# Earlier short-convolution taps, earlier bonus sums and earlier first statistics in a hybrid RWKV-7 / attention / PEER step

## The chip, the cores and the metric

The kernel runs on one core of one Trainium2 chip. The metric is the device time of one execution in microseconds (us). The kernel before was timed three times: 3184.2, 3185.47 and 3186.89 us, a median of 3185.47 us. One more execution was recorded by the hardware profiler, and all rows below come from it.

The engines are TensorE (PE, matmuls, with its weight loads shown as PEld), VectorE (DVE), ScalarE (ACT), GpSimd (POOL) and SyncE (SP). Each executes its own instructions in program order. They wait for each other through semaphores: `then_inc(name, 1)` counts up when an instruction is done, and `wait_ge(name, n)` holds an engine until the count is reached.

## The reference

One step of a two-layer model for 128 context tokens and 256 latent tokens of width 1024. Layer 0 mixes tokens with a bidirectional RWKV-7 scan beside a short gated convolution, layer 1 with differential attention. Each mixer is followed by a PEER expert retrieval. The parts that the change touches are these:

```python
def short_conv(bg, cg, hc, conv_w):
    z = cg * hc
    zp = jnp.pad(z, ((0, 0), (1, 1), (0, 0)))
    y = zp[:, 0:T] * conv_w[0] + zp[:, 1:T + 1] * conv_w[1] + zp[:, 2:T + 2] * conv_w[2]
    return bg * y

# in rwkv7_bidir, for each of the two directions d
kd = heads(k * (1 + (a - 1) * k_a))
s_fin, o = wkv_scan(s0[:, d], rh, decay, kd, vh, kk, heads(a), d == 1)
bons.append(jnp.sum(rh * kd * r_k.astype(f32), axis=-1, keepdims=True) * vh)
# after both: group norm of the outputs, plus bons[0] + bons[1], times the gate

# around the mixer
hp = rmsnorm(xp, norm_mix[l]) * (1 + sc1p) + sh1p      # the same for xs
xp = xp + g1p * yp
hp = rmsnorm(xp, norm_ffn[l]) * (1 + sc2p) + sh2p      # statistics of the updated x
xp = xp + g2p * peer(hp, peer_w_q[l], ...)
```

## The kernel before, in words

The 384 tokens are three tiles of 128 (t = 0 context, t = 1 and 2 latent). All weights pass through one SBUF ring of four slots, 512 KB a tile, in a fixed order that SP follows. SP reloads a slot when its tile is used: for tiles that are split in a high and a low part (input projection, query, experts) when DVE has made the low part (`low`), for the others when PE has multiplied them. `high(g)` on ACT waits for the landing of tile g and copies it to `w_hi`, and `low(g)` on DVE makes the rest `w_lo`.

Layer 0 goes through these stages:

- The input projection of 26 column bands (`project`, `take_projection`). For each band PE does 24 matmuls, and ACT copies the result to `proj`. Between bands, ACT, DVE and PE run the pieces of `rwkv_prep(n)`, which makes decays, normalised keys and the vectors KAP, BET, GAM, RHO of both directions. ACT calls its piece n after taking band n, DVE calls its piece n after `low` of band n. The bands come in the order `MIX0`, which ends with `CG`, `HC` (the convolution's inputs), `BG` and the gate's lora band.
- The scan (`rwkv_units`). There are six units q (a direction and a token tile each). In each, `levels(q)` inverts a triangular system in six levels lv. At each level PE makes a product, DVE masks it (`PM`), PE multiplies again, DVE subtracts from `XM` and transposes it, and the next level can start. The function `between(q, lv, s)` on every engine hangs other work into this chain at step (lv, s): the matrices of the next unit, pairs of adaLN weight tiles on PE (`ada_pair`), and in unit 0 the short convolution and the bonus.
- The output rows (`even_rows`) on PE, the residual updates (`after_mix`) on DVE, and on ACT the sums of squares for the next norm (`norm_stats_by_half`), which visits six half tiles in the order `ROWS_MIX[0]`: (0,0), (1,0), (0,1), (0,2), (1,1), (1,2) as (half nb, tile t). DVE needs the root of tile 0 for `normalise(1, 0)`, which it calls ahead of the third residual.
- The second norm: PE transposes `xn` (`norm_T`), ACT and DVE scale and split it (`norm_evac`), the query projection follows, then the experts.

The convolution before is made in unit 0: DVE's product z = CG * HC at step (1,0), ACT's centre tap at (1,1), DVE's first outer taps at (2,0), its second outer taps at (4,2), and the product with BG at (5,2). The bonus sum kd[0] + kd[1], times r, is made by DVE at (1,2) and scaled by r_k on ACT at (2,0); PE needs it at (4,0).

Of the kernel before, what the change touches and what calls it, by code (L numbers as in the profile page):

```python
# [21 lines left out]
ALU = mybir.AluOpType  # L22
ACT = mybir.ActivationFunctionType
AX_X = mybir.AxisListType.X

P = 128
# [7 lines left out]
NF = 4  # L34
# [94 lines left out]
def build(nc, A):  # L129
    with ExitStack() as ctx:  # L130
# [1106 lines left out]
        def _(act):  # L1237
# [30 lines left out]
            def norm_stats_by_half(n, rows):  # L1268

                seen = set()  # L1270
                for k, (nb, t) in enumerate(rows):
                    cols = slice(512 * nb, 512 * nb + 512)
# [48 lines left out]
            def rwkv_prep(n):  # L1321
# [31 lines left out]
                if 12 <= n < 18:  # L1353
# [7 lines left out]
                    if k == 2:  # L1361
                        act.activation(dec[d], half[d], ACT.Exp, scale=-c).then_inc(exp_ready, 1)

            def rwkv_units():
# [12 lines left out]
                def between(q, lv, s):  # L1377

                    at = (lv, s)
                    if q == 0 and at == (1, 1):  # L1380
                        act.wait_ge(conv_z, 1)
                        for f in range(NF):
                            act.activation(proj[:, HC + f, :], proj[:, CG + f, :], ACT.Copy, scale=ft("conv", 4 + f)).then_inc(conv_y, 1)
                    if q == 0 and at == (2, 0):
                        act.wait_ge(rkd_sum, 1)
                        for f in range(NF):
                            ins = act.activation(kd[0][:, f, :], kd[0][:, f, :], ACT.Copy, scale=ft("r_k", f))
                        ins.then_inc(rkd_ready, 1)
# [171 lines left out]
            for layer in range(2):  # L1560
# [12 lines left out]
                for n in range(2):  # L1573
                    high(at["query"] + n)
                norm_stats_by_half(2 * layer + 1, ROWS_MIX[layer])
# [10 lines left out]
        def _(dve):  # L1586
# [143 lines left out]

            def rwkv_prep(n):
# [61 lines left out]
                if n in (21, 24):  # L1793
                    rho_kappa((n - 21) // 3)

            def rwkv_units():
# [146 lines left out]
                def taps(w, lo):  # L1943

                    z, y = proj[:, CG:CG + NF, :], proj[:, HC:HC + NF, :]
                    for f in range(NF):
                        for a, b in ((0, P), (P, T)):
                            out = y[:, f, a + 1:b] if lo else y[:, f, a:b - 1]
                            src = z[:, f, a:b - 1] if lo else z[:, f, a + 1:b]
                            ins = dve.scalar_tensor_tensor(out, src, ft("conv", w + f), out, ALU.mult, ALU.add)  # L1950
                    chained(ins)

                def short_conv(at):

                    z, y = proj[:, CG:CG + NF, :], proj[:, HC:HC + NF, :]
                    if at == (1, 0):
                        tt(z, z, y, ALU.mult).then_inc(conv_z, 1)
# [527 lines left out]
```

## Time and profile before

| quantity | value |
|---|---|
| median of three runs | 3185.47 us |
| profiled execution, whole time | 3189.87 us |
| its span (first to last instruction) | 3188.0 us |
| PE busy | 3065.4 us, 96% |
| DVE busy | 2029.4 us, 64% |
| ACT busy | 1147.5 us, 36% |
| mean granted TensorE clock | 0.988 of full |

The profiled execution took 4.40 us longer than the median of the runs, and its span leaves out 1.87 us of it. Times of rows are us from the start of the span. In the rows of instructions in order of time, a bracket is the idle time of the engine ahead of the group and what ended it. The input projection ends at about 167 us, unit 0 of the scan reaches to about 214 us, the scan to about 435 us, and the query projection of layer 0 starts at about 480 us.

### The profile page before, as it was taken

What the parts mean: (1) busy time and instruction counts of PE and PEld (TensorE: products, weight loads), DVE (VectorE), ACT (ScalarE), POOL (GpSimd) and SP (SyncE); (2) the same over time, 40 slices, a digit from 0 to 9 for tenths busy, and PEclk for the clock granted to TensorE, in tenths of its full rate; (3) what the DMA queues carried; (4) which work ended last, traced back from release to release, by engine and by line L of the source; (5) the groups of instructions that cost most, each with busy time, mean ns of one, the idle gap of its engine ahead of it and who ended that gap; (6) DMA issues with size and microseconds to landing.
All of it is one profiled execution on the core that took longest, in us unless ns stands there. A gap on an engine that the chain in (4) does not pass through costs nothing.

```text
span 3188.0 us, 51951 instructions
## 1 busy us (share of the span) xinstructions
PE 3065.4 (96%) x20266; PEld 2689.6 (84%) x20266; DVE 2029.4 (64%) x4372; ACT 1147.5 (36%) x1552; POOL 11.2 (0%) x23
## 2 busy tenths in 40 slices
PE   7989889999999999999999979999999999999998
PEld 4956649999999998888888868999999998888887
DVE  3875554687878436666666474587878625666666
ACT  4611113454545432222223264345454532222222
POOL 0000000000000000000000000000000000000000
PEclk9999999999999999999999989999999999999999
DMA  6345533566665856766763313456565765766763
GB/s 229 112 160 205 184 119 124 155 207 192 201 196 189 285 159 204 235 214 211 237 206 122 111 46 120 127 180 214 178 218 181 232 226 179 237 213 211 238 204 132
DMA packets 281942, 589.16 MB, mean 185 GB/s; under 512 B 17744, under 2 KB 181712, under 8 KB 275360
## 3 DMA queue, kind: packets, MB, share of 16 engines
q1 hardware_dynamic: 140960, 428.57, 40.8%
q10 hardware_dynamic: 139008, 151.00, 14.3%
q0 software_dynamic: 1792, 7.01, 0.6%
q8 instruction: 132, 2.16, 0.3%
q14 instruction: 50, 0.41, 0.0%
HBM read 482.97 MB, written 103.55 MB: 184 GB/s over the span
## 4 chain that ended last, share of the span: by engine, by line
PE 88%; DVE 7%; DMA 2%; issue 1%; ACT 1%; SPq 0%; ACTq 0%; DVEq 0%
PE ps L1182 33%; PE ps L580 13%; PE ps L582 13%; PE ps L581 13%; PE ps L1158 4%; DVE arena L1596 3%; DMA ring<-in_ada 2%; PE ps L553 1%; PE ps L690 1%; PE ps L641 1%; DVE w_lo L1596 1%; PE ps L1131 1%; PE ps L672 1%; PE ps L757 1%; PE ps L607 0%
## 5 line engine op out<-in xcount | busy, mean ns | idle before, releaser
L1596 DVE TENSOR_TENSOR w_lo<-ring,w_hi 128x1024 fp32r<-128x1024 f32 x576 | 702.2, 1221 | 344.9 <-ACT w_hi L1251 344.0
L580 PE MATMUL ps<-hT_hi,w_hi 128*128 128x384 f32 x2576 | 873.5, 339 | 3.0 <-ACT arena L1524 3.0
L581 PE MATMUL ps<-hT_lo,w_hi 128*128 128x384 f32 x2576 | 861.4, 334 | 0.0
L582 PE MATMUL ps<-hT_hi,w_lo 128*128 128x384 f32 x2384 | 797.8, 335 | 0.0
L1251 ACT ACTIVATE w_hi<-ring 128x1024 fp32r<-128x1024 f32 x378 | 400.0, 1060 | 964.6 <-PE ps L582 791.9
L1182 PE MATMUL ps<-w_lo,ga_hi 128*128 128x512 f32 x1512 | 596.6, 395 | 0.0
L1182 PE MATMUL ps<-w_hi,ga_lo 128*128 128x512 f32 x1512 | 596.6, 395 | 0.0
L1182 PE MATMUL ps<-w_hi,ga_hi 128*128 128x512 f32 x1512 | 596.6, 395 | 0.0
L580 PEld LDWEIGHTS ps<-hT_hi,w_hi 128*128 128x128 f32 x2576 | 484.1, 188 | 6.4 <-issue 5.9
L1544 ACT ACTIVATE w_hi<-ring 128x1024 fp32r<-128x1024 f32 x224 | 238.2, 1063 | 697.9 <-PE ps L1182 634.5
L1596 DVE TENSOR_TENSOR arena<-arena 128x768 bf16<-128x768 bf16 (+10 forms) x937 | 422.6, 511 | 99.5 <-PE ps L1158 94.3
L581 PEld LDWEIGHTS ps<-hT_lo,w_hi 128*128 128x128 f32 x2576 | 484.5, 188 | 0.5
L582 PEld LDWEIGHTS ps<-hT_hi,w_lo 128*128 128x128 f32 x2384 | 448.0, 188 | 0.0
L2306 DVE CAST ga_hi<-xn 128x384 fp32r<-128x384 f32 x256 | 92.5, 361 | 423.4 <-PE ps L1182 408.1
L1182 PEld LDWEIGHTS ps<-w_hi,ga_lo 128*128 128x128 f32 x1512 | 284.9, 188 | 66.5
L1182 PEld LDWEIGHTS ps<-w_lo,ga_hi 128*128 128x128 f32 x1512 | 284.9, 188 | 66.4
L1182 PEld LDWEIGHTS ps<-w_hi,ga_hi 128*128 128x128 f32 x1512 | 284.9, 188 | 66.3
L1508 ACT ACTIVATE arena<-ps 128x512 f32<-128x512 f32 x192 | 192.5, 1105 | 1.4 <-PE ps L1158 1.0
L1158 PE MATMUL ps<-arena 128*128 128x128 bf16 x2304 | 150.8, 219 | 6.1 <-DVE arena L1596 5.6
L1158 PEld LDWEIGHTS ps<-arena 128*128 128x128 bf16 x2304 | 133.1, 97 | 23.1 <-issue 14.2
L1596 DVE TENSOR_TENSOR ga_lo<-xn,ga_hi 128x384 fp32r<-128x384 f32 x256 | 143.0, 559 | 8.9
L1596 DVE TENSOR_TENSOR xn<-arena 128x384 f32<-128x384 f32 (+2 forms) x274 | 147.4, 541 | 0.3
(313 smaller groups left out, 2147.9 us busy)
## 6 DMA issues: line engine op xcount, KB each, us to landing
ring<-in_u SPq DMA_DIRECT2D x256, 512.0 KB, 3.8
ring<-in_v SPq DMA_DIRECT2D x256, 512.0 KB, 3.4
ring<-in_ada SPq DMA_DIRECT2D x96, 512.0 KB, 4.8
act_dram<-arena SPq DMA_DIRECT2D x256, 192.0 KB, 3.9
g_dram<-arena ACTq DMA_DIRECT2D x48, 1024.0 KB, 4.1
arena<-g_dram ACTq DMA_DIRECT2D x32, 1536.0 KB, 9.6
arena<-act_dram ACTq DMA_DIRECT2D x32, 1536.0 KB, 15.6
ring<-in_mix_in SPq DMA_DIRECT2D x42, 512.0 KB, 3.3
```

Of the source, the lines that this page charges most:

```text
L553: mm = pe.matmul(ps[g:g + 8, 6, :], silu8[:, c, b, :], w[:, 512 * cc:512 * cc + 512], start=(b == 0 and c < 4), stop=(b == 3 and c >= 4))
L580: pe.matmul(out, hi[:, c, :], hT_hi[:, c, :], start=(c == 0), stop=False)
L581: pe.matmul(out, hi[:, c, :], hT_lo[:, c, :], start=False, stop=False)
L582: mm = pe.matmul(out, lo[:, c, :], hT_hi[:, c, :], start=False, stop=(c == DC - 1))
L641: mm = pe.matmul(ps[:, 3 * nb + t, :], l_[:, c, ts], r_[:, cc, :], start=(c == 0 and m == 0), stop=(c == DC - 1 and m == 2))
L1158: mm = pe.matmul(ps[:, k, q * P:(q + 1) * P], hot_u[n % 3][:, q // 2, :, q % 2], gated_hot[n % 3][:, q // 2, w, :, q % 2], start=(w == 0), ...
L1182: mm = pe.matmul(ps[:, 2 * t + nb, :], l_[:, n % 2, ts], r_[:, cs], start=(first and q == 0), stop=False, skip_group_check=True)
L1251: act.activation(w_hi[:, g % WB, :], ring[:, g % RING, :], ACT.Copy).then_inc(hi_ready, 1)
L1508: act.activation(gstage[:, b, :, 4 * q:4 * q + 4].rearrange("p j t -> p t j"), ps[:, k, :].rearrange("p (t j) -> p t j", t=4), ACT.Copy).t ...
L1544: act.activation(w_hi[:, g % WB, :], ring[:, g % RING, :], ACT.Copy).then_inc(hi_ready, 1)
L1596: return dve.tensor_tensor(out, a, b, op)
L2306: dve.tensor_copy(ga_hi[:, k % 2, :], ga[:, k % 2, :]).then_inc(ga_high, 1)
```

## The change

Three things move. No operation is added or removed.

1. The convolution's product z, its centre tap and its first outer taps leave unit 0 and become pieces of `rwkv_prep`: DVE makes z in piece 24 and the taps in piece 25, ACT makes the centre tap in piece 23.
2. The bonus sums leave unit 0 as well: DVE makes them in piece 25, and ACT scales them in piece 24.
3. In layer 0, ACT takes the statistics of tile 0 first, and copies the first two query tiles (`high`) behind them. In layer 1 the order stays.

```diff
-            def norm_stats_by_half(n, rows):
+            def norm_stats_by_half(n, rows, highs_at=None, highs=()):
                 seen = set()
                 for k, (nb, t) in enumerate(rows):
+                    if k == highs_at:
+                        for g in highs:
+                            high(g)
...
+                if n == 23:
+                    act.wait_ge(conv_z, 1)
+                    for f in range(NF):
+                        act.activation(proj[:, HC + f, :], proj[:, CG + f, :], ACT.Copy, scale=ft("conv", 4 + f)).then_inc(conv_y, 1)
+                if n == 24:
+                    act.wait_ge(rkd_sum, 1)
+                    for f in range(NF):
+                        ins = act.activation(kd[0][:, f, :], kd[0][:, f, :], ACT.Copy, scale=ft("r_k", f))
+                    ins.then_inc(rkd_ready, 1)
...
-                    if q == 0 and at == (1, 1):
-                        act.wait_ge(conv_z, 1)
...
-                    if q == 0 and at == (2, 0):
-                        act.wait_ge(rkd_sum, 1)
...
-                for n in range(2):
-                    high(at["query"] + n)
-                norm_stats_by_half(2 * layer + 1, ROWS_MIX[layer])
+                norm_stats_by_half(2 * layer + 1, ROWS_MIX[layer], 0 if layer else 2, [at["query"], at["query"] + 1])
...
+                if n == 24:
+                    dve.wait_ge(proj_taken, 21)
+                    tt(proj[:, CG:CG + NF, :], proj[:, CG:CG + NF, :], proj[:, HC:HC + NF, :], ALU.mult).then_inc(conv_z, 1)
+                if n == 25:
+                    chained(tt(kd[0], kd[0], kd[1], ALU.add))
+                    tt(kd[0], kd[0], proj[:, R_:R_ + NF, :], ALU.mult).then_inc(rkd_sum, 1)
+                    dve.wait_ge(conv_y, NF)
+                    taps(0, 1)
...
-                    if at == (1, 0):
-                        tt(z, z, y, ALU.mult).then_inc(conv_z, 1)
-                    if at == (2, 0):
-                        dve.wait_ge(conv_y, NF)
-                        taps(0, 1)
...
-                        if at == (1, 2):
-                            chained(tt(kd[0], kd[0], kd[1], ALU.add))
-                            tt(kd[0], kd[0], proj[:, R_:R_ + NF, :], ALU.mult).then_inc(rkd_sum, 1)
```

The first place is the end of the projection. On DVE, before, the last low part (`w_lo_m`) is the last work ahead of the scan, whose first instruction writes `gate_bc`:

```order
L1596 TENSOR_TENSOR w_lo_m<-ring,w_hi 128x1024 [waits hi_ready]
L1596 TENSOR_TENSOR arena<-arena 128x1536 [waits proj_taken]
L1596 TENSOR_TENSOR arena<-arena,xn 128x1536
L1596 TENSOR_TENSOR w_lo_m<-ring,w_hi 128x1024 [waits hi_ready]
L1596 TENSOR_TENSOR gate_bc<-const 128x64 [waits prep_done,levels_in,proj_taken]
```

Now z stands ahead of that low part, and the bonus sums (written to `xn`) and eight tap instructions, of which the first two are shown, stand behind it:

```order
L1597 TENSOR_TENSOR w_lo_m<-ring,w_hi 128x1024 [waits hi_ready]
L1597 TENSOR_TENSOR arena<-arena 128x1536 [waits proj_taken]
L1597 TENSOR_TENSOR arena<-arena,xn 128x1536
L1597 TENSOR_TENSOR arena<-arena 128x1536 [waits proj_taken]
L1597 TENSOR_TENSOR w_lo_m<-ring,w_hi 128x1024 [waits hi_ready]
L1597 TENSOR_TENSOR xn<-xn,arena 128x1536
L1597 TENSOR_TENSOR xn<-xn,arena 128x1536 [waits dve_order]
L1739 SCALAR_TENSOR_TENSOR arena<-arena,feats 128x127 [waits conv_y]
L1739 SCALAR_TENSOR_TENSOR arena<-arena,feats 128x255
```

On ACT at the same place, now, the two groups of four scalings stand between the copies of the last bands (L1320 takes a band, L1387 is the scan's first work):

```order
L1320 ACTIVATE arena<-ps 128x384 [waits multiplied] x2
L1369 ACTIVATE arena<-arena,feats 128x384 [waits conv_z]
L1369 ACTIVATE arena<-arena,feats 128x384 x3
L1320 ACTIVATE arena<-ps 128x384 [waits multiplied]
L1373 ACTIVATE xn<-xn,feats 128x384 [waits rkd_sum]
L1373 ACTIVATE xn<-xn,feats 128x384 x3
L1320 ACTIVATE arena<-ps 128x384 [waits multiplied]
L1387 ACTIVATE arena<-ps 128x512 [waits turn_ready,proj_taken]
```

Before, the same stretch of ACT had only the copies of the bands, and the scalings came in the scan (`ACT L1383`, `L1387`).

The second place is unit 0 of the scan on DVE, from the masked product of level 1 to the subtraction of level 2 (`hslab` holds the unit's matrices). Before:

```order
L1596 TENSOR_TENSOR arena<-ps,gate_bc 128x128 [waits fill_ready] x2
L1596 TENSOR_TENSOR arena<-arena 128x1536
L1596 TENSOR_TENSOR hslab<-hslab,ps 128x64x2 [waits fill_ready] x2
L2055 STREAM_TRANSPOSE hslab<-hslab 128x256 [waits fill_taken]
L2058 STREAM_TRANSPOSE hslab<-hslab 64x256 [waits fill_taken]
L2058 STREAM_TRANSPOSE hslab<-hslab 64x256
L1596 TENSOR_TENSOR xn<-xn,arena 128x1536
L1596 TENSOR_TENSOR xn<-xn,arena 128x1536 [waits dve_order]
L1596 TENSOR_TENSOR arena<-ps,gate_bc 128x128 [waits fill_ready] x2
L1950 SCALAR_TENSOR_TENSOR arena<-arena,feats 128x127 [waits conv_y]
```

Now:

```order
L1597 TENSOR_TENSOR arena<-ps,gate_bc 128x128 [waits fill_ready] x2
L1597 TENSOR_TENSOR hslab<-hslab,ps 128x64x2 [waits fill_ready] x2
L2055 STREAM_TRANSPOSE hslab<-hslab 128x256 [waits fill_taken]
L2058 STREAM_TRANSPOSE hslab<-hslab 64x256 [waits fill_taken]
L2058 STREAM_TRANSPOSE hslab<-hslab 64x256
L1597 TENSOR_TENSOR arena<-ps,gate_bc 128x128 [waits fill_ready] x2
L1597 TENSOR_TENSOR hslab<-hslab,ps 128x32x4 [waits fill_ready] x2
```

Nothing but the chain of the levels is left between the two subtractions.

The third place is ACT between the end of the scan (the root of the last group norm) and the third half tile's statistics. Before, the two copies of query tiles (`w_hi<-ring`) come first:

```order
L1427 ACTIVATE xn<-ps,feats 128x512 [waits gn_ready]
L1251 ACTIVATE w_hi<-ring 128x1024 [waits multiplied,weight_landed2]
L1251 ACTIVATE w_hi<-ring 128x1024 [waits multiplied,weight_landed3]
L1275 ACTIVATE xn,stat<-x 128x512 [waits x_updated]
L1278 ACTIVATE stat<-stat,feats 128x1 [waits act_order]
L1275 ACTIVATE xn,stat<-x 128x512 [waits x_updated,act_order]
L1280 ACTIVATE stat<-stat 128x1 [waits act_order]
```

Now the four instructions on tile 0 come first:

```order
L1430 ACTIVATE xn<-ps,feats 128x512 [waits gn_ready]
L1278 ACTIVATE xn,stat<-x 128x512 [waits x_updated]
L1281 ACTIVATE stat<-stat,feats 128x1 [waits act_order]
L1278 ACTIVATE xn,stat<-x 128x512 [waits x_updated,act_order]
L1283 ACTIVATE stat<-stat 128x1 [waits act_order]
L1251 ACTIVATE w_hi<-ring 128x1024 [waits multiplied,weight_landed2]
L1251 ACTIVATE w_hi<-ring 128x1024 [waits multiplied,weight_landed3]
```

The landings of two query tiles are no longer waited for ahead of tile 0's root, but still ahead of the statistics of tiles 1 and 2.

## Rows read from the trace of the kernel before

**Rows 1.** The page's chain that ended last, by engine, shares of the span.

```profile
PE 88%; DVE 7%; DMA 2%; issue 1%; ACT 1%; SPq 0%; ACTq 0%; DVEq 0%
```

**Rows 2.** DVE in order of time, projection's end: start, us, instructions, idle before.

```profile
155.13 1.75 DVE L1596 TENSOR_TENSOR arena<-arena,xn 128x1536 f32<-128x1536 f32 x1
156.80 1.22 DVE L1596 TENSOR_TENSOR w_lo_m<-ring,w_hi 128x1024 fp32r<-128x1024 f32 x1
167.41 0.22 DVE L1596 TENSOR_TENSOR gate_bc<-const 128x64 f32<-128x64 f32 x1 [9.39 <-ACT arena L1317]
```

**Rows 3.** ACT in order of time, last band and the scalings.

```profile
166.89 0.49 ACT L1317 ACTIVATE arena<-ps 128x384 f32<-128x384 f32 x1 [3.67 <-PE ps L582]
...
179.68 2.13 ACT L1383 ACTIVATE arena<-arena,feats 128x384 f32<-128x384 f32 x4 [6.19 <-DVE arena L1596]
184.95 2.13 ACT L1387 ACTIVATE xn<-xn,feats 128x384 f32<-128x384 f32 x4 [3.14 <-DVE xn L1596]
```

**Rows 4.** DVE in order of time, unit 0, levels 1 and 2.

```profile
177.89 1.75 DVE L1596 TENSOR_TENSOR arena<-arena 128x1536 f32<-128x1536 f32 x1
179.56 0.48 DVE L1596 TENSOR_TENSOR hslab<-hslab,ps 128x128 f32<-128x128 f32 x2
...
181.37 3.55 DVE L1596 TENSOR_TENSOR xn<-xn,arena 128x1536 f32<-128x1536 f32 x2
184.84 0.48 DVE L1596 TENSOR_TENSOR arena<-ps,gate_bc 128x128 f32<-128x128 f32 x2
185.24 2.70 DVE L1950 SCALAR_TENSOR_TENSOR arena<-arena,feats 128x127 f32<-128x127 f32 x8
187.97 0.48 DVE L1596 TENSOR_TENSOR hslab<-hslab,ps 128x128 f32<-128x128 f32 x2
```

**Rows 5.** PE in order of time, unit 0, levels 1 to 3.

```profile
178.12 0.67 PE L817 MATMUL ps<-arena,hslab 64*64 64x32 f32 x32 [1.13 <-DVE arena L1596]
180.18 0.67 PE L804 MATMUL ps<-hslab 64*64 64x32 f32 x32 [1.39 <-DVE hslab L1596]
180.78 1.86 PE L553 MATMUL ps<-ring,gate_bc 128*8 128x512 f32 x8
185.42 1.08 PE L817 MATMUL ps<-arena,hslab 64*64 64x32 f32 x32 [2.78 <-DVE arena L1596]
...
193.52 0.67 PE L817 MATMUL ps<-arena,hslab 64*64 64x32 f32 x32 [0.64 <-DVE arena L1596]
```

**Rows 6.** The chain that ended last, in order of time: start, us, what.

```profile
191.72 4.76 DMA ring<-in_ada
```

**Rows 7.** Stretches: length, PE, PEld, DVE, ACT, POOL busy (instructions), PEclk, DMA share, GB/s.

```profile
181.00:191.00 10.00, 7.22 (x68) 3.60 (x60) 9.81 (x20) 3.54 (x7) 0.00 (x0) 0.50 0.30 107
468.00:477.00 9.00, 3.28 (x16) 3.28 (x16) 7.57 (x16) 5.33 (x15) 0.00 (x0) 0.50 0.35 117
```

**Rows 8.** ACT in order of time, after the scan of layer 0.

```profile
461.14 1.06 ACT L1251 ACTIVATE w_hi<-ring 128x1024 fp32r<-128x1024 f32 x1 [2.43 <-DMA ring<-in_query]
...
463.92 0.29 ACT L1280 ACTIVATE stat<-stat 128x1 f32<-128x1 f32 x1
```

**Rows 9.** DVE in order of time, residuals and norm.

```profile
464.32 0.16 DVE L1620 RECIPROCAL stat<-stat 128x1 f32<-128x1 f32 x1 [10.11 <-ACT stat L1280]
...
465.31 0.68 DVE L1596 TENSOR_TENSOR arena<-ps,gate_bc 128x512 f32<-128x512 f32 x1
...
474.29 0.88 DVE L1624 TENSOR_SCALAR xn<-x,stat 128x512 f32<-128x512 f32 x2
```

**Rows 10.** PE in order of time, output rows, transposes, first query matmul.

```profile
443.95 20.77 PE L672 MATMUL ps<-ring,arena 128*128 128x512 f32 x48
465.06 1.09 PE L595 MATMUL ps<-const,xn 128*128 128x128 f32 x8 [0.34 <-DVE xn L1624]
473.72 3.65 PE L595 MATMUL ps<-const,xn 128*128 128x128 f32 x16 [7.57 <-DVE xn L1624]
479.62 0.44 PE L607 MATMUL ps<-hT_hi,w_hi 128*128 128x384 f32 x1 [2.25 <-DVE hT_lo L1596]
```

More of the change, by code:

```diff
@@ L1379, in between @@
                     at = (lv, s)
-                    if q == 0 and at == (1, 1):
-                        act.wait_ge(conv_z, 1)
-                        for f in range(NF):
-                            act.activation(proj[:, HC + f, :], proj[:, CG + f, :], ACT.Copy, scale=ft("conv", 4 + f)).then_inc(conv_y, 1)
-                    if q == 0 and at == (2, 0):
-                        act.wait_ge(rkd_sum, 1)
-                        for f in range(NF):
-                            ins = act.activation(kd[0][:, f, :], kd[0][:, f, :], ACT.Copy, scale=ft("r_k", f))
-                        ins.then_inc(rkd_ready, 1)
                     if q == 3 and at == (4, 0) or q == 5 and at == (3, 0):
@@ L1729, in low, with taps @@
                 tt(lo, ring[:, g % RING, :], hi.bitcast(F32), ALU.subtract).then_inc(lo_ready[TILES[g][0]], 1)
+            def taps(w, lo):
+                z, y = proj[:, CG:CG + NF, :], proj[:, HC:HC + NF, :]
+                for f in range(NF):
+                    for a, b in ((0, P), (P, T)):
+                        out = y[:, f, a + 1:b] if lo else y[:, f, a:b - 1]
+                        src = z[:, f, a:b - 1] if lo else z[:, f, a + 1:b]
+                        ins = dve.scalar_tensor_tensor(out, src, ft("conv", w + f), out, ALU.mult, ALU.add)
+                chained(ins)
             def rwkv_prep(n):
@@ L1941, in bonus @@
                     tt(proj[:, R_ + f, :], filled()[:, 0:T], proj[:, V_ + f, :], ALU.mult).then_inc(fill_taken, 1)
[L1943 to L1951, printed above, removed]
-                def short_conv(at):
-                    z, y = proj[:, CG:CG + NF, :], proj[:, HC:HC + NF, :]
-                    if at == (1, 0):
-                        tt(z, z, y, ALU.mult).then_inc(conv_z, 1)
-                    if at == (2, 0):
-                        dve.wait_ge(conv_y, NF)
-                        taps(0, 1)
+                def short_conv(at):
                     if at == (4, 2):
@@ L1963, in short_conv @@
                     if at == (5, 2):
-                        tt(proj[:, BG:BG + NF, :], proj[:, BG:BG + NF, :], y, ALU.mult).then_inc(conv_done, 1)
+                        tt(proj[:, BG:BG + NF, :], proj[:, BG:BG + NF, :], proj[:, HC:HC + NF, :], ALU.mult).then_inc(conv_done, 1)
                 def between(q, lv, s):
```

## The prediction

> **What bounds the kernel now.** I read the page's chain of waits first: PE carries 88% of it, DVE 7% and DMA 2% [rows 1]. So a DVE or ACT instruction only counts where PE stands idle for it. The changed code runs in two such places, and I read each in order of time on PE, DVE and ACT.
>
> In unit 0 of the scan DVE is never idle between 177.9 and 188 us, while PE has gaps of 1.39 and 2.78 us that DVE ends [rows 4, 5]. In the 10 us from 181 to 191, DVE is busy 9.81 us and PE 7.22, at a granted clock of 0.50, the lower level of 1.2 GHz [rows 7]. DVE bounds this stretch, and the work to be moved stands in it. Ahead of it, at the end of the projection, DVE is idle for 9.39 us until ACT has taken the last band [rows 2].
>
> After the scan DVE is idle for 10.11 us until ACT has made tile 0's root, and ACT got to it late because its copy of the second query tile waited for the landing until 461.14 [rows 8, 9]. PE finishes the output rows at 464.72 and then has a gap of 7.57 us between the transposes of tile 0 and those of tile 1 [rows 10].
>
> **Part 1, where the work goes to.** DVE's z takes 1.67 us of its time (177.89 to 179.56), the bonus sums 3.47 (181.37 to 184.84), the taps 2.73 (185.24 to 187.97), in all 7.87 us [rows 4]. At the projection's end, z now starts at 156.80 and ends at 158.5, and the last low part follows at 158.5 to 159.6. PE needs that one at 162.7 (one band's 4.16 us ahead of the last band's end, 3.67 + 0.49 in [rows 3]), so 3 us are left. The bonus sums run to about 163.1 (+3.5) and the taps to 165.8 (+2.7), where DVE's first scan instruction could not start before 167.41 anyway [rows 2]. The 9.39 us of idle time hide the 7.87, with 1.6 us to spare.
>
> ACT has two groups of four scalings of 2.13 us each [rows 3]. Bands are taken at 158.57, 162.73 and 166.89 (4.16 apart). The first group follows band 23's copy at 159.05, when z is ready since 158.5, and ends at 161.2, ahead of band 24. The second waits for the bonus sums at 163.1, just when band 24's copy is done (163.2), and ends at 165.4, 1.5 us ahead of the last band. Behind that wait stands the copy of the last band, and PE, DVE and ACT all start the scan on it. Beyond 1.5 us, each us of delay would cost one. I cost this at nothing.
>
> **Part 1, what it removes.** All else up to PE's product at 178.12 stays. It ends at 178.79, and DVE can subtract at 178.83 instead of 179.56 [rows 4, 5]. From there to the next DVE step behind the transposes it is 1.81 us (179.56 to 181.37), so the transposes end at 180.6. PE's next product starts at 179.45 (0.14 behind the subtraction's end, as 180.18 stands behind 180.04) and its pair of adaLN tiles at 180.05. DVE's masked product of level 2 starts at 180.6 instead of 184.84 and ends at 181.1. PE's second product then starts at 181.2 to 181.4 instead of 185.42, which the idle 2.78 us and the DVE work before it had held.
>
> From here the price depends on PE's clock. The product took 1.08 us at the lower level, and 0.67 at the full one [rows 5]. DVE's subtraction of level 2 starts at 181.9 (full) or 182.4 (half) instead of 187.97, 6.0 or 5.5 us earlier. To PE's product of level 3 at 193.52 it is 5.55 us of DVE work in both. The second brake is the ring: the transfer in the chain takes 4.76 us from 191.72, behind the second pair of tiles, and ends in a PE start at about 196.5 [rows 6]. That pair would be done at 184.6 instead of 191.3 with the full clock (6.7 earlier), at about 186 with half the clock for a few us (5.3), and at about 187 if the level stayed low as long after PE has become dense as before (from 185.42 to 191, [rows 5, 7]), which gives 4.2. Upper end 6.0, lower end 4.2. Before the drop PE now has the adaLN pair and two products close together, so I expect a shorter stretch at half clock, but not none: I take 5.2 us. Behind level 3 the order is as before, so the scan shifts by this as a whole, its own transfers with it.
>
> **Part 2.** The first two residuals are done at 454.21 (464.32 less 10.11 idle, [rows 9]). ACT's statistics of one half tile take 1.05 us (463.92 + 0.29 less the second copy's end at 462.1, halved, [rows 8]), so tile 0's root is ready at 455.4. PE does six output tiles in 20.77 us, 3.46 each [rows 10]: the fourth is half done at 456.0 and done at 457.8, the sixth done at 464.72. DVE therefore normalises tile 0 at 456.0 (1.0 us), and the residuals three and four (1.35 us each, 465.31 less 464.32 being the norm's 0.99) end at 459.8.
>
> The query copies on ACT wait for the same landings as before: at 457.65 (the copy that ended at 458.71 took 1.06) and 461.14 [rows 8]. DVE's low parts follow at 459.8 and 462.2, the second ending at 463.4. Residual five (PE's part is there at 463.0) ends at 464.8, residual six waits for PE's 464.72 and ends at 466.2. ACT has done the statistics three and four at 464.2, takes five at 464.8 and six at 466.2, ready at 467.3. DVE's last normalisation then starts at 467.5 instead of 474.29 and ends at 468.4: 6.8 us earlier. What is late next is no longer a landing but PE's own last output tile, with a tail of residual, square, root and scaling.
>
> PE gains a little more. Its 16 transposes took 3.65 us at a clock of 0.50, 0.228 each, against 1.09 us for 8 before it, 0.136 each [rows 7, 10], and DVE waited for them. With PE's idle stretches now about 1 us between tile 0's and tile 1's transposes, they should run at the full clock, and DVE can scale at once behind its own normalisation: 469.15, split 1.6 us later, low part 0.9, first query matmul at 471.8 instead of 479.62, that is 7.8 us. Lower end: the clock still falls, and besides the first query matmuls run at half clock for about the 3.7 us of dense work that it took to rise (473.72 to some 477.4, [rows 7, 10]), losing 1.85, and the transposes 0.2: 5.8. I take 7.8.
>
> A rule speaks against this. In [rows 7, 10] PE did nothing but transposes from 473.72 on, and by 478 the clock was full when the first query matmul came at its usual pace. The Trainium skill, "TensorE: Matmul & The Clock Gate", section "Part 4: PE-mode transpose", says that transposes don't count as busy time for the clock in the same way as matmuls; by it, PE would look idle from 464.72 to 471.8 and the gain would be the 5.8 us. The rows side with the transposes counting.
>
> **The sum.** 5.2 + 7.8 = 13.0 us. The profiled execution's 3189.87 us becomes 3176.9; against the median, which is 4.40 us lower, 3185.47 becomes 3172.5 us. All that follows (experts, layer 1) is the same order of work, started earlier. Three runs lay within 2.7 us, so 0.2% (6.4 us) is about what can be told from no change.
>
> **The rivals.**
> - *The ring takes the scan's gain back.* For: a transfer of 4.76 us is in the chain of unit 0 [rows 6], and with less DVE work the same tiles are wanted faster. Against: the next pairs keep their distance, since the order behind level 3 is unchanged. If the tiles pace unit 0, part 1 is worth 1 us: 3185.47 - 8.8 = 3176.7. Chance 0.13.
> - *The clock falls at the query projection after all.* Part 2 is worth 5.8: 3174.5. Chance 0.12.
> - *The second query tile lands late.* ACT now waits for it ahead of tiles 1 and 2. It was there at 461.14, and from about 462 on DVE's low part holds residual five. For: the wait on the landing is the one that ended last before. Against: PE's last output tile ends only at 464.72. A landing 2.4 us later costs 2.4 us: 3174.9. Chance 0.06.
> - *The last band is held behind the bonus sums, and it is slower than before.* For: all three engines start the scan on that band, and ACT now waits ahead of it. Against: the sum above has the sums ready at 163.1, and it decides from 164.8 on. It would be slower by 0.2% only if they came at about 184 (164.8 + 13.0 + 6.4), so DVE would have to be 21 us behind: 3192. Chance 0.02.
> - *One of the moves does nothing.* If ACT's root was late for another reason than the landing, only part 1 is left: 3180.3. Chance 0.05; [rows 8] speaks against it.
>
> **How the numbers follow.** My forecast, both gains within their ends, has 0.62 and gives 3172.5 us, with 3170.5 to 3175.5 from its own ends. The range for 8 in 10 reaches to the ring's rival and some us beyond both ends, for the scatter of the run: 3168 to 3179. Faster by over 0.2% means below 3179.1: all of the forecast and most of the first three rivals, 0.90. Within 0.2%: 0.07, the last rival and the tail. Slower: 0.03.
>
> **What would show it.** Right: PE's level 2 product in unit 0 about 4 us earlier, no scalings on ACT within the scan's unit 0, DVE's idle time ahead of the scan down to about 1.6 us, and the first scan product still at 167.4. After the scan, DVE's 10 us wait for ACT's root gone, PE's gap of 7.57 us down to about 1, and the first query matmul some 13 us earlier than 479.62. Wrong: a scan that starts after 168, PE waits for `ring<-in_ada` that grow by several us, a clock below full at the first query matmuls, or a later stretch that gives the time back.

## The result, and the profile after

The changed kernel takes 3173.3 us, the median of five runs, against 3185.47 us before (five runs here, the same median as before). The ratio of the runs is 0.9953, with a 95% interval of 0.9941 to 0.9965: 15 us faster by the ratio, 11 to 19 by its interval, 12.2 by the medians. The forecast was 3172.5. The profiled execution has a span of 3172.7 us, 15.3 less than before. Of the experiments' executions further down, three (one of e7 at 6998 us, two of the kernel before at 10570 and 10590 us) took two to three times as long as the others and are left out of the ratios.

Where the 15.3 us come from, read from the start times of the same instructions in both traces:

| stretch | before | after | less |
|---|---|---|---|
| start to the last band's copy on ACT | 166.89 | 164.24 | 2.6 |
| from there to PE's level 5 product L830, unit 0 | 43.5 | 39.4 | 4.1 |
| from there to the first output row L672 (units 1 to 5) | 224.9 | 220.0 | 4.9 |
| from there to the first query matmul L607 | 44.3 | 36.8 | 7.5 |
| from there to the first expert-sum matmul L1182 | 695.4 | 698.6 | -3.2 |
| the rest | 2013.0 | 2013.7 | -0.7 |

These are the rows of PE that the second and third line are read from (before, then now):

```profile
210.40 1.15 PE L830 MATMUL ps<-const,hslab 64*64 64x64 f32 x32
435.30 3.60 PE L672 MATMUL ps<-ring,arena 128*128 128x512 f32 x8
```

```profile
203.66 1.15 PE L830 MATMUL ps<-const,hslab 64*64 64x64 f32 x32
423.64 3.60 PE L672 MATMUL ps<-ring,arena 128*128 128x512 f32 x8
```

Only the second and the fourth line are stretches that got shorter by the moved code, and they repeat with it in the experiments below. The first has moved code at its end, but its 2.6 us are older than that: the band copy at 102.94 us before starts at 100.29 now, some 50 us ahead of the first moved instruction. The other lines have the same code in the same order.

At the projection's end the moved work lies as in the prediction. These are DVE's instructions in order of time in the changed kernel (start, us, instruction, and in brackets the idle time before), the answer to [rows 2]:

```profile
154.14 1.75 DVE L1597 TENSOR_TENSOR arena<-arena 128x1536 f32<-128x1536 f32 x1
155.81 1.22 DVE L1597 TENSOR_TENSOR w_lo_m<-ring,w_hi 128x1024 fp32r<-128x1024 f32 x1
156.94 3.54 DVE L1597 TENSOR_TENSOR xn<-xn,arena 128x1536 f32<-128x1536 f32 x2
160.40 2.71 DVE L1739 SCALAR_TENSOR_TENSOR arena<-arena,feats 128x127 f32<-128x127 f32 x8
164.82 0.22 DVE L1597 TENSOR_TENSOR gate_bc<-const 128x64 f32<-128x64 f32 x1 [1.70 <-issue]
```

The idle time of 9.39 us is down to 1.70, and DVE's first scan instruction starts 0.58 us behind the start of the last band's copy, against 0.52 before. ACT's scalings, the answer to [rows 3], lie between the bands, and what the copies of the bands wait for is PE (the bracket), not one of them:

```profile
156.30 2.13 ACT L1369 ACTIVATE arena<-arena,feats 128x384 f32<-128x384 f32 x4
160.07 0.49 ACT L1320 ACTIVATE arena<-ps 128x384 f32<-128x384 f32 x1 [1.64 <-PE ps L582]
160.52 2.14 ACT L1373 ACTIVATE xn<-xn,feats 128x384 f32<-128x384 f32 x4
164.24 0.49 ACT L1320 ACTIVATE arena<-ps 128x384 f32<-128x384 f32 x1 [1.58 <-PE ps L582]
```

In unit 0, PE's instructions in order of time answer to [rows 5]:

```profile
172.47 2.08 PE L757 MATMUL ps<-arena 64*128 64x128 f32 x16 [0.76 <-DVE hslab L1597]
174.48 1.08 PE L804 MATMUL ps<-hslab 64*64 64x32 f32 x32
176.38 1.08 PE L817 MATMUL ps<-arena,hslab 64*64 64x32 f32 x32 [0.82 <-DVE arena L1597]
178.13 1.08 PE L804 MATMUL ps<-hslab 64*64 64x32 f32 x32 [0.67 <-DVE hslab L1597]
179.14 1.89 PE L553 MATMUL ps<-ring,gate_bc 128*8 128x512 f32 x8
180.97 1.08 PE L817 MATMUL ps<-arena,hslab 64*64 64x32 f32 x32
...
187.65 0.67 PE L817 MATMUL ps<-arena,hslab 64*64 64x32 f32 x32 [1.01 <-DVE arena L1597]
```

The level 2 product (180.97) has lost its wait of 2.78 us. But all of these products up to it run at half clock: 1.08 us where the same instruction takes 0.67 in the last line, and 2.08 where it takes 1.16 elsewhere in the trace. Counted from the last band's copy, the level 2 product stands at 16.73 us instead of 18.53, and the level 3 product (187.65) at 23.41 instead of 26.63. The stretches of the changed kernel (length, busy time of PE, PEld, DVE, ACT, POOL, PEclk, DMA share, GB/s) show it beside [rows 7]:

```profile
168.00:172.00 4.00, 2.58 (x36) 2.06 (x32) 3.90 (x9) 1.76 (x3) 0.00 (x0) 1.00 0.01 4
172.00:183.00 11.00, 9.03 (x164) 6.79 (x166) 6.28 (x18) 0.00 (x0) 0.00 (x0) 0.53 0.08 26
183.00:193.00 10.00, 8.98 (x174) 4.53 (x174) 9.03 (x23) 1.19 (x2) 0.00 (x0) 1.00 0.86 324
```

DVE is busy 6.28 us of the 11 from 172 to 183, where it had been busy 9.81 of 10: it no longer bounds that part of unit 0, PE at half clock does.

After the scan, DVE's wait for ACT's root is gone. Its rows in order of time answer to [rows 9]:

```profile
441.86 0.69 DVE L1597 TENSOR_TENSOR x<-x,arena 128x512 f32<-128x512 f32 x1
444.51 0.16 DVE L1621 RECIPROCAL stat<-stat 128x1 f32<-128x1 f32 x1 [1.96 <-PE ps L672]
...
451.13 1.23 DVE L1597 TENSOR_TENSOR w_lo<-ring,w_hi 128x1024 fp32r<-128x1024 f32 x1 [1.75 <-ACT w_hi L1251]
452.27 0.68 DVE L1597 TENSOR_TENSOR arena<-ps,gate_bc 128x512 f32<-128x512 f32 x1
...
456.32 0.88 DVE L1625 TENSOR_SCALAR xn<-x,stat 128x512 f32<-128x512 f32 x2
```

What ends DVE's idle time at 444.51 is now PE's own output row. The landing is still waited for, on ACT, whose rows answer to [rows 8]:

```profile
443.40 0.29 ACT L1283 ACTIVATE stat<-stat 128x1 f32<-128x1 f32 x1
445.92 1.06 ACT L1251 ACTIVATE w_hi<-ring 128x1024 fp32r<-128x1024 f32 x1 [2.23 <-DMA ring<-in_query]
450.04 1.06 ACT L1251 ACTIVATE w_hi<-ring 128x1024 fp32r<-128x1024 f32 x1 [3.06 <-DMA ring<-in_query]
```

And PE's rows answer to [rows 10]:

```profile
434.44 18.62 PE L672 MATMUL ps<-ring,arena 128*128 128x512 f32 x43
452.89 1.04 PE L595 MATMUL ps<-const,xn 128*128 128x128 f32 x8
455.74 2.21 PE L595 MATMUL ps<-const,xn 128*128 128x128 f32 x16 [1.81 <-DVE xn L1625]
460.41 0.44 PE L607 MATMUL ps<-hT_hi,w_hi 128*128 128x384 f32 x1 [2.46 <-DVE hT_lo L1597]
```

The gap of 7.57 us is 1.81, and the 16 transposes take 2.21 us instead of 3.65.

### The profile page after: what moved, and what is told of

Its sections match the earlier page's. It is cut to its first block, busy times and chain, and to the rows that moved or that the text cites. A ratio compares the mean times of both kernels' runs of the same rounds, so it can differ in the third digit from the quotient of the medians.

```text
span 3172.7 us, 51951 instructions
## 1 busy us (share of the span) xinstructions
PE 3059.1 (96%) x20266; PEld 2685.3 (85%) x20266; DVE 2028.2 (64%) x4372; ACT 1147.0 (36%) x1552; POOL 11.2 (0%) x23
## 3 DMA queue, kind: packets, MB, share of 16 engines
q1 hardware_dynamic: 140960, 428.57, 40.2%
## 4 chain that ended last, share of the span: by engine, by line
PE 88%; DVE 7%; DMA 2%; ACT 1%; issue 1%; ACTq 0%; SPq 0%; DVEq 0%
PE ps L1182 33%; PE ps L580 13%; PE ps L581 13%; PE ps L582 13%; PE ps L1158 4%; DVE arena L1597 4%; DMA ring<-in_ada 2%; PE ps L553 1%; PE ps L690 1%; PE ps L641 1%; DVE w_lo L1597 1%; PE ps L1131 1%; PE ps L672 1%; PE ps L757 1%; PE ps L817 0%
## 5 line engine op out<-in xcount | busy, mean ns | idle before, releaser
L1182 PE MATMUL ps<-w_hi,ga_hi 128*128 128x512 f32 x1512 | 596.8, 395 | 0.0
L1182 PE MATMUL ps<-w_hi,ga_lo 128*128 128x512 f32 x1512 | 596.8, 395 | 0.0
L1182 PE MATMUL ps<-w_lo,ga_hi 128*128 128x512 f32 x1512 | 596.7, 395 | 0.0
L1182 PEld LDWEIGHTS ps<-w_hi,ga_hi 128*128 128x128 f32 x1512 | 285.0, 188 | 66.5
L1182 PEld LDWEIGHTS ps<-w_hi,ga_lo 128*128 128x128 f32 x1512 | 285.0, 188 | 66.3
L1182 PEld LDWEIGHTS ps<-w_lo,ga_hi 128*128 128x128 f32 x1512 | 285.0, 188 | 66.2
```

Of the source, the lines that this page charges most:

```text
L1182: mm = pe.matmul(ps[:, 2 * t + nb, :], l_[:, n % 2, ts], r_[:, cs], start=(first and q == 0), stop=False, skip_group_check=True)
```

## The experiments

Ratios are to the kernel before, run beside each experiment. Because the intervals are 0.11 to 0.16% to each side, 4 to 5 us, the argument rests on stretches of the traces. The table has four of them for every kernel, in us: L3, from the last band's copy on ACT to PE's level 3 product in unit 0, behind which only the second outer taps (e5, e8) move; U0, from the same copy to PE's level 5 product in unit 0; U1-5, from there to the first output row; N, from there to the first score matmul of the experts (L1131), which contains the norm and the whole query projection. "Half" is the time that TensorE's clock was at half within U0 and within U1-5, read from the granted clock in stretches of 1 us. Each kernel has one profile, so each row is one execution.

| kernel | L3 | U0 | U1-5 | N | half, U0 / U1-5 | ratio, 95% interval |
|---|---|---|---|---|---|---|
| before | 26.6 | 43.5 | 224.9 | 115.7 | 10 / 7 | |
| changed | 23.4 | 39.4 | 220.0 | 108.1 | 10 / 0 | 0.9953, 0.9941 to 0.9965 |
| e1, scan part | 22.1 | 38.6 | 221.7 | 115.6 | 3 / 3 | 0.9987, 0.9972 to 1.0001 |
| e2, statistics part | 26.6 | 43.2 | 221.6 | 111.1 | 10 / 3 | 0.9969, 0.9955 to 0.9982 |
| e3, convolution only | 25.3 | 42.8 | 222.0 | 117.1 | 10 / 7 | 0.9991, 0.9976 to 1.0006 |
| e4, bonus only | 23.3 | 40.2 | 220.8 | 118.1 | 7 / 7 | 0.9983, 0.9971 to 0.9994 |
| e5, second taps too | 21.3 | 37.3 | 220.0 | 111.6 | 3 / 7 | 0.9958, 0.9943 to 0.9973 |
| e6, sums late | 23.2 | 39.7 | 229.5 | 109.1 | 7 / 27 | 0.9963, 0.9948 to 0.9977 |
| a1, changed again | 22.3 | 39.3 | 221.3 | 108.3 | 7 / 0 | 0.9955, 0.9941 to 0.9968 |
| e7, dense PE | 21.8 | 37.6 | 232.8 | 111.1 | 0 / 24 | 0.9947, 0.9933 to 0.9962 |
| e8, e5 and e7 | 21.8 | 37.6 | 229.5 | 109.2 | 0 / 17 | 0.9954, 0.9938 to 0.9969 |

From L3 to the end of U0 the kernels take 15.8 to 17.5 us, with no order that follows the changes.

**e1: the scan part alone.** The changed kernel, with its third part taken back:

```diff
-                norm_stats_by_half(2 * layer + 1, ROWS_MIX[layer], 0 if layer else 2, [at["query"], at["query"] + 1])
+                norm_stats_by_half(2 * layer + 1, ROWS_MIX[layer], 0, [at["query"], at["query"] + 1])
```

Expected:

> Only the moves of the convolution and of the bonus sums to the projection's end; ACT copies the two query tiles ahead of the statistics as before. My theory: unit 0 of the scan is bounded by DVE, the moved 7.9 us are hidden in its idle stretch of 9.4 us, and unit 0 is 4 to 5 us shorter; all later units only shift. Against before: 4 to 6 us faster. Rival (the rest of the gap between 4 us in unit 0 and 9 us at the scan's end in the changed kernel's trace belongs to this part, through fewer waits for adaLN tiles): 8 to 9 us faster. Rival (the ring takes it back): 0 to 2 us. DVE still waits 10 us for ACT's root after the scan in all three.

Measured: 0.9987, that is 4 us, from 9 faster to no gain. Unit 0 is 4.9 us shorter, N is as before. After the scan the old wait is back. These are PE's rows there:

```profile
454.14 1.09 PE L595 MATMUL ps<-const,xn 128*128 128x128 f32 x8 [0.27 <-DVE xn L1625]
462.80 3.65 PE L595 MATMUL ps<-const,xn 128*128 128x128 f32 x16 [7.57 <-DVE xn L1625]
```

Time and trace agree with the 4 to 5 us of unit 0. The interval leaves out neither rival by itself, and includes no gain; that the ring takes the gain back is answered by the trace, in which unit 0 keeps it.

**e2: the statistics part alone.** The kernel before, with the third hunk of the change only:

```diff
-                for n in range(2):
-                    high(at["query"] + n)
-                norm_stats_by_half(2 * layer + 1, ROWS_MIX[layer])
+                norm_stats_by_half(2 * layer + 1, ROWS_MIX[layer], 0 if layer else 2, [at["query"], at["query"] + 1])
```

Expected:

> Only the statistics of tile 0 ahead of the two query copies in layer 0; the scan as before. My theory: 7.5 us faster than before, with PE's first query matmul 15 us after its last output-row matmul became 7.4 us after it. Rival (the clock falls at the query projection without the scan's gain, or a late landing): 5 to 6 us. The scan, from the last band's copy to the first output row, is 268 us as before.

Measured: 0.9969, 10 us (6 to 14). With e1's 4 us that makes 14, so the ratios of the two parts add up to the 15 of the whole. The gap on PE is gone, but in the profiled execution the clock fell all the same:

```profile
463.68 3.60 PE L595 MATMUL ps<-const,xn 128*128 128x128 f32 x16 [2.00 <-DVE xn L1625]
469.56 0.44 PE L607 MATMUL ps<-hT_hi,w_hi 128*128 128x384 f32 x1 [2.29 <-DVE hT_lo L1597]
```

The mean granted clock of e2 from 463 to 467 us was 0.59 (the third number from the end):

```profile
463.00:467.00 4.00, 3.32 (x16) 3.26 (x16) 2.66 (x9) 3.31 (x9) 0.00 (x0) 0.59 0.81 312
```

The transposes took 3.60 us instead of 2.21, and the first query matmul stands 8.8 us behind the last output row, where I had expected 7.4 and the changed kernel has it. N is 4.6 us shorter than before, where the changed kernel's is 7.5. This is the rival of 5 to 6 us, in this execution. Also, units 1 to 5 took 221.6 us, 3.3 less than before, though not one instruction of the scan is different; the 268 us that I had expected from the last band to the first output row were 264.8. So most of the 4.9 us in the third line of the first table need no change to explain them.

**e3 and e4: the halves of the scan part.** e3 moves only the convolution's pieces, e4 only the bonus sums; in both the statistics stay as before. In e3, against e1, the sums go back on DVE (and their scaling on ACT):

```diff
                 if n == 25:
-                    chained(tt(kd[0], kd[0], kd[1], ALU.add))
-                    tt(kd[0], kd[0], proj[:, R_:R_ + NF, :], ALU.mult).then_inc(rkd_sum, 1)
...
+                        if at == (1, 2):
+                            chained(tt(kd[0], kd[0], kd[1], ALU.add))
+                            tt(kd[0], kd[0], proj[:, R_:R_ + NF, :], ALU.mult).then_inc(rkd_sum, 1)
```

e4 is the kernel before with the same lines moved the other way:

```diff
+                if n == 25:
+                    chained(tt(kd[0], kd[0], kd[1], ALU.add))
+                    tt(kd[0], kd[0], proj[:, R_:R_ + NF, :], ALU.mult).then_inc(rkd_sum, 1)
```

Expected of e3:

> Only the convolution product, its centre tap and its first outer taps moved (4.4 us of DVE), bonus sums and statistics as before. My theory (DVE bounds unit 0): z gives 0.7 us (PE's product was 0.7 us away), the taps 1.5 to 2.7; against before 2 to 3.5 us faster, PE's product of level 3 in unit 0 stands 24 to 25 us behind the last band's copy instead of 26.6. Rival (only what reaches beyond the next PE wait counts, and the ring takes the rest): under 1 us.

Expected of e4:

> Only the bonus sums and their scaling moved (3.5 us of DVE), convolution and statistics as before. My theory: the sums stood directly ahead of the masked product of level 2, so nearly all of the 3.5 us counts: 2.5 to 3.5 us faster than before. Rival (the taps behind them cannot start earlier because of ACT's centre tap, or PE is next): 1 us. Band 26's copy on ACT is not late: DVE's sums end about 2 us earlier than in the full change since z does not stand ahead of them.

Measured: unit 0 is 0.7 us shorter in e3 and 3.3 in e4; together 4.0, the 4.1 of the full change. At level 3 the two are 1.3 us (189.97 - 164.68 = 25.3 against 26.6) and 3.4, together 4.7, where e1 has 4.5. So in e3, 4.4 us of DVE work gave 1.3 us, under what I expected, and from level 3 to level 5 this execution was the slowest of all. DVE's rows of e3 show where it waits instead:

```profile
181.91 0.48 DVE L1597 TENSOR_TENSOR arena<-ps,gate_bc 128x128 f32<-128x128 f32 x2
183.61 0.49 DVE L1597 TENSOR_TENSOR hslab<-hslab,ps 128x128 f32<-128x128 f32 x2 [1.22 <-PE ps L817]
...
185.61 1.29 DVE L1597 TENSOR_TENSOR arena<-ps,const 128x512 f32<-128x512 f32 x2 [0.21 <-PE ps L757]
...
189.20 0.49 DVE L1597 TENSOR_TENSOR arena<-ps,gate_bc 128x128 f32<-128x128 f32 x2 [0.47 <-PE ps L804]
```

The taps had stood where DVE now waits 1.22 us for PE's product, so at half clock they were partly free already. The bonus sums had stood directly ahead of a masked product whose input was ready, and nearly all of their 3.5 us counted. The ratios, 3 us faster than before for e3 (from 8 faster to 2 slower) and 5 for e4 (2 to 9), do not tell the two apart.

**e5: the second outer taps at the projection's end too.** Against the changed kernel:

```diff
                     taps(0, 1)
+                    taps(8, 0)
...
-                    if at == (4, 2):
-                        taps(8, 0)
```

Expected:

> The changed kernel, with the second outer taps (2.7 us of DVE, unit 0, level 4) moved to the projection's end as well, behind the first. Theory: the idle 1.7 us that are left there plus the 1.2 us in which DVE waits for PE's first scan products hide the 2.7, and unit 0 is up to 2.7 us shorter behind level 4: 1.5 to 2.7 us faster than the changed kernel, so 14 us faster than before. Rival (cover used up: the scan starts later by what is moved beyond 1.7 us, and level 4 has slack or waits for tiles): same as the changed kernel within 1 us.

Measured: U0 is 37.3 us, 2.1 less than the changed kernel and 2.0 less than its second profile, but the ratio 0.9958 is that of the changed kernel. DVE's rows at the start of the scan:

```profile
160.84 5.46 DVE L1739 SCALAR_TENSOR_TENSOR arena<-arena,feats 128x127 f32<-128x127 f32 x16
166.33 0.23 DVE L1597 TENSOR_TENSOR gate_bc<-const 128x64 f32<-128x64 f32 x1
166.47 1.28 DVE L1597 TENSOR_TENSOR hslab<-ps,const 128x512 f32<-128x512 f32 x2
```

DVE has no idle time left there, and its first masked product starts 1.80 us behind the last band's copy (at 164.67) instead of 1.73 (165.97 after 164.24). So the second taps are hidden. But that they also shorten unit 0, as I expected, is not shown. The level 3 product stands 21.3 us behind the last band's copy, 1.0 us less than in a1 and 2.1 less than in the changed kernel's profile, and up to there the scan's code is the same. In this execution the clock was at half for 3 us of unit 0, against 7 and 10. Behind level 3, where the second taps had stood, e5 takes 16.0 us to the end of U0, the changed kernel 16.0 and a1 17.0. And e8, which has these taps moved, and e7, which has not, both at full clock, have the same L3 and the same U0. These are their products of level 3 and of level 5, first e7 (last band's copy at 164.32), then e8 (at 167.01):

```profile
186.16 0.67 PE L819 MATMUL ps<-arena,hslab 64*64 64x32 f32 x32 [0.19 <-DVE arena L1607]
...
201.94 1.15 PE L834 MATMUL ps<-const,hslab 64*64 64x64 f32 x32
```

```profile
188.86 0.67 PE L819 MATMUL ps<-arena,hslab 64*64 64x32 f32 x32 [0.61 <-DVE arena L1607]
...
204.66 1.15 PE L834 MATMUL ps<-const,hslab 64*64 64x64 f32 x32
```

That fits the rival that level 4 has slack: in e7 the taps (2.71 us) still stand in level 4, and the DVE instruction behind them waits for nothing, yet PE's product of level 5 comes no earlier without them.

**e6: the sums behind the taps.** Against the changed kernel:

```diff
-                    chained(tt(kd[0], kd[0], kd[1], ALU.add))
-                    tt(kd[0], kd[0], proj[:, R_:R_ + NF, :], ALU.mult).then_inc(rkd_sum, 1)
                     dve.wait_ge(conv_y, NF)
                     taps(0, 1)
+                    chained(tt(kd[0], kd[0], kd[1], ALU.add))
+                    tt(kd[0], kd[0], proj[:, R_:R_ + NF, :], ALU.mult).then_inc(rkd_sum, 1)
```

Expected:

> The changed kernel, but in piece 25 the taps come ahead of the bonus sums. Theory (the last band's copy stands behind ACT's wait for the sums, and all engines start the scan on it): the sums end 4.3 us later than in the changed kernel, ACT's scaling ends 2.6 us later than the last band is ready, the scan starts 2.6 us late, and the kernel is 2 to 2.6 us slower than the changed one (10 us faster than before). Rival (DVE or the ring bounds the scan's start anyway): no difference from the changed kernel.

Measured, first on ACT, then on PE:

```profile
161.40 0.49 ACT L1320 ACTIVATE arena<-ps 128x384 f32<-128x384 f32 x1 [1.65 <-PE ps L582]
166.12 2.13 ACT L1373 ACTIVATE xn<-xn,feats 128x384 f32<-128x384 f32 x4 [4.23 <-DVE xn L1597]
168.16 0.47 ACT L1320 ACTIVATE arena<-ps 128x384 f32<-128x384 f32 x1
```

```profile
165.19 0.34 PE L582 MATMUL ps<-hT_hi,w_lo_m 128*128 128x384 f32 x1
168.68 1.30 PE L757 MATMUL ps<-arena 64*128 64x128 f32 x16 [3.15 <-ACT arena L1320]
```

The last band is copied at 168.16, 4.16 + 2.60 us behind the band before, so 2.6 us late, and PE idles 3.15 us where it idled 0.58. The mechanism of my slower rival exists: the sums came 4.3 us later, and what went beyond the reserve of 1.6 us delayed the band one for one. U0 does not show it, since it is counted from the late copy; from the copy of the band before, PE's level 5 product stands at 46.4 us instead of 43.6. The ratio, 0.9963, is 3 us above the changed kernel's, and their intervals overlap.

**a1, e7 and e8: the spread, and a dense PE.** a1 is the changed kernel once more. e7 adds 22 matmuls whose results nobody reads, in PE's gaps of unit 0's start; e8 is e5 with the same.

```diff
+                def fill_gap(n):
+                    for _ in range(n):
+                        pe.matmul(ps[:, 7, 0:P], ident, ones, start=True, stop=True)
...
                 row(0, 2)
+                fill_gap(7)
                 products(0, BET, RHO)
+                fill_gap(4)
                 products(0, GAM, RHO)
...
+                        if q == 0 and lv == 1:
+                            fill_gap(7)
...
+                        if q == 0 and lv == 1:
+                            fill_gap(4)
```

Expected of a1:

> The changed kernel once more, with nothing altered, for the spread of its stages between executions. Theory: what is one us per cause (projection's end, units 1 to 5 of the scan, the late expert stage) moves by 1 to 4 us from one execution to the next at the same code, because TensorE's clock falls at other times; unit 0 from the last band's copy to PE's product of level 5 takes 38.5 to 39.5 us, and the first query matmul follows the first output-row matmul by 36.7 to 38.3. Rival: all stages repeat within 0.5 us, and the 5 us that units 1 to 5 took less in the changed kernel's trace belong to the change. Time: 12 us faster than before.

Expected of e7:

> The changed kernel with 22 more matmuls of 128 columns on PE in the gaps in which it waits for DVE at the start of unit 0; their results are not used. Theory (the clock falls in unit 0 because PE is thinly used from 170 to 178 us, and the low stretch costs 1 to 2 us): the clock stays at its full level through unit 0, the product of level 3 stands 21 to 22 us behind the last band's copy instead of 23.4, and the kernel is 0 to 2 us faster than the changed one. Rival (the extra matmuls delay the chain by their own length, or the clock falls all the same): same or 1 to 2 us slower.

Expected of e8:

> The changed kernel with the second outer taps at the projection's end and with the 22 extra matmuls. Theory: both gains add, unit 0 is 3 to 4 us shorter than in the changed kernel, 2 to 4 us faster in time. Rival (noise of the later stages hides it): the stage is shorter, but the time differs by under 1 us.

Measured: a1 repeats U0 and N within 0.2 us, and units 1 to 5 within 1.3. Its first query matmul stands 36.9 us behind the first output row. So the two profiles of the changed kernel alone do not refute the rival for units 1 to 5, in which both are under the 224.9 before; what speaks against it is e2, which is nearly as short with the old scan. In e7 the clock stays full through unit 0:

```profile
164.00:202.00 38.00, 36.83 (x632) 23.65 (x631) 29.56 (x73) 4.86 (x8) 0.00 (x0) 1.00 0.51 170
```

U0 is 37.6 us, 1.7 to 1.8 less than in the changed kernel and a1. That is what is left after the matmuls' own price: they delay DVE's first subtraction to 13.0 us behind the last band's copy, where a1, at full clock up to there, has 11.9. The level 3 product came at 21.8, within the 21 to 22 expected. e8 missed its expectation: the two gains do not add, U0 is 37.6 again and not 3 to 4 us shorter than the changed kernel's.

Units 1 to 5 took 232.8 us in e7 and 229.5 in e8, with 12.0 us of PE waits for adaLN tiles in each, where the changed kernel had 4.8 and a1 5.7. By the time, e7 (0.9947) and e8 (0.9954) are no better than a1 (0.9955) run beside them. e6, without extra matmuls, also took 229.5 us in units 1 to 5, with 4.2 us of such waits. What the three long profiles share is the clock: at half for 17 to 27 us of this stretch, against 0 to 7 in the eight others. They are also the slowest executions counted for their kernels (3185.8 us in e6, 3178.9 in e7, 3178.6 in e8). Whether the extra matmuls of e7 and e8 have a part in the longer tile waits and the clock's falls is open.

No version was found that the runs show to be faster than the changed kernel.

## Why the prediction was right, and where a step was off

The forecast of 13.0 us stands against 12.2 by the medians and 15 by the ratio. Both mechanisms were named rightly. That the number is so close is in part luck: the two terms came out at 4.1 and 7.5 us in the changed kernel's profile, 11.6 together, and the profiled pair got to 15.3 only through stretches whose code is the same (2.6 and 4.9 us less, 3.2 and 0.7 more). For the same reason the first query matmul came 19.2 us earlier, where 13 was forecast, and the first scan product at 164.8, where 167.4 was. Step by step:

- *The moved work is hidden at the projection's end.* Right. 1.70 us of idle time were left on DVE where 1.6 were forecast, ACT's last band waits for PE alone, and e6 shows what stood behind the reserve.
- *Unit 0 gets 5.2 us shorter (4.2 to 6.0).* The mechanism was right and the term somewhat too big. At PE's level 3 product, to which the sum was made, it was 3.2 us in the profile, 4.4 in a1 and 4.5 in e1; at level 5 it was 4.1, 4.2 and 4.9. PE's level 2 product, forecast about 4 us earlier, was 1.8 us earlier in the profile and 3.1 in a1 and e1, counted from the last band. The step that failed was "all else up to PE's product at 178.12 stays". In the profiled execution the clock was at half from about 172 us, ahead of the places that the moved code had left, and DVE's first subtraction came 13.26 us behind the last band (177.50 - 164.24) where it had been 12.67 before and should have been 11.9. In e1 it was 11.95 (176.10 - 164.15). In e6, where the clock was full from the first subtraction on, and in e5, where it fell only just ahead of the level 2 product, that product stood 14.5 us behind the last band's copy, and the sum has 14.3 to 14.5. So the order of work was right, and what was mis-sized is the half clock. I expected a shorter stretch of it; in the changed kernel's profile it began 8 us behind the last band's copy instead of 14 and lasted the same 10 us, while in a1 and e1 it lasted 7 and 3, and there level 3 is within the range of the forecast. e7, with no half clock in unit 0, shows what it costs: 1.7 to 1.8 us of U0, after the delay by e7's own extra matmuls.
- *The split of that term.* I had counted z, sums and taps alike as DVE work on the path. e3 and e4, one profile each, put 3.4 us of it at level 3 on the sums (3.3 at level 5) and 1.3 (0.7) on the convolution's pieces, with 4.4 us of work.
- *The ring takes it back.* Not in unit 0: PE's waits for adaLN tiles there were 0.2 us before, none in the changed kernel, 0.2 in a1 and 0.8 in e1. In units 1 to 5 the trace of the changed kernel has fewer such waits than before (4.8 us against 7.9), e2 5.8 with the old scan, so no effect of the change is seen there.
- *Behind unit 0 everything only shifts.* Right in the order of work, wrong as a statement on one pair of traces. Units 1 to 5 took 220.0 to 224.9 us in eight of eleven profiles and 229.5 to 232.8 in three, and code that did not change gave 4.9 us in my pair. The kernel before has a single profile, with 7 us at half clock in this stretch; that a us or two of the 4.9 come with the change is not ruled out, since its two profiles (220.0 and 221.3) are among the shortest. Later, 3.2 us were lost again, late in the experts' first stage: PE waited 2.2 us for ACT there and ran at half clock for a few us behind it, against a wait of 0.5 before. e2 has the same wait with 2.5 us, but a1 has 1.0 in two pieces, e5 0.5, and e6, e7 and e8 have none. So it varies between executions of the new order; what starts it is open.
- *The statistics part gives 7.8 us (lower end 5.8).* The wait and its removal were right: 7.5 in the profile, from 44.3 to 36.8. The size rests on a full clock, and that held only in the changed kernel's profile and in a1. In the five other profiles with the new order (e2, e5, e6, e7, e8) the clock fell there and the 16 transposes took 3.08 to 3.60 us instead of 2.21. From the first output row to the first query matmul the seven take 36.8 to 38.2 us (mean 37.6) and the four with the old order 44.2 to 44.3, so the gain is 6.1 to 7.5, 6.6 on the average. N says the same with more spread: 108.1 to 111.6 (mean 109.8) against 115.6 to 118.1 (mean 116.6), so 6.8. The rival that the clock falls at the query projection after all, with a chance of 0.12, was thus the usual case.
- *The second query tile lands late.* In a small way: ACT's second copy came at 450.04, 26.40 us behind the first output row, against 25.84 before (461.14 - 435.30), and DVE's residual five started at 452.27, some 0.5 us later than the sum had it. The sixth then could not start with PE's last row.
- *The transposes and the clock.* In the changed kernel the clock was full over 453 to 461 us, in which PE did only the eight transposes (from 452.89) and the 16, with the first matmul at 460.41:

```profile
453.00:461.00 8.00, 3.68 (x28) 2.99 (x27) 7.70 (x16) 7.00 (x18) 0.00 (x0) 1.00 0.53 197
```

By the Trainium skill's rule ("TensorE: Matmul & The Clock Gate", section "Part 4: PE-mode transpose") that transposes do not count as busy time in the same way, this stretch should look idle. The trace does not agree, and a1's has the same full clock. In e2 the clock did fall with a like load, at about 463.7, so these two are no proof by themselves. But it rose again at about 467.1, when PE had done nothing but transposes since 463.68, as it rose in the kernel before at about 477.8, with nothing but transposes since 473.72. PE's gap ahead of the 16 was 1.8 to 2.1 us in the seven profiles, where about 1 was forecast.

## What to carry to other kernels

Work that is moved out of a chain between two engines only counts where the next step's input was ready: ask of each piece what the engine would have waited for without it. The sums (3.5 us of work) gave 3.4, z and the first taps (4.4 us) 1.3, the second taps (2.7 us) nothing that a profile shows. And an engine that waits for a landing must not stand ahead of short work that others wait for: putting four small instructions ahead of two copies was worth 6 to 7.5 us. Before a difference between two single traces is explained, look at a stage whose code did not change: here such a stage moved by 5 us.

## What was not expected of the hardware

TensorE's clock fell to half in different places at the same code. In unit 0 it was at half from about 181 to 191 us before, from 172 to 183 in the changed kernel, and from 177 to 184 in a1, with full clock through the unit only when PE's gaps were filled (e7 and e8). This moved single steps by 1.1 to 1.4 us (the level 3 product of unit 0 between the changed kernel and a1, the 16 transposes between e2 and a1). It goes with the spread of several us between executions of equal code: the three profiles with the longest units 1 to 5 are those with the most time at half clock.
